# VectorE's order in the expert loop: the low part of half-chunk 10 placed behind the clip and SwiGLU of the second half

## The chip, the cores and the metric

The kernel runs on one core of a Trainium2 chip. The metric is the device time of one execution in microseconds, from its first to its last instruction with what lies around them. Times of a kernel are medians of several executions; the profile is one execution more.

## What is computed

One layer of a decoder, for 512 prompt tokens and 32 sample tokens (8 sequences of 4) that share the weights: windowed attention, a short convolution and memory attention side by side, then a mixture of experts with 32 experts, four of them for each token, then a last norm. The part around the change is the expert layer:

```python
def expert_block(args):
    xb, e = args
    h = xb @ w_gate_up[e] + b_gate_up[e]
    gate = jnp.minimum(h[:, 0::2], SWIGLU_LIMIT)
    up = jnp.clip(h[:, 1::2], -SWIGLU_LIMIT, SWIGLU_LIMIT)
    glu = gate * jax.nn.sigmoid(gate * SWIGLU_ALPHA)
    return ((up + 1.0) * glu) @ w_down[e] + b_down[e]
```

The model width and the width of the expert's hidden layer are both 1024. Weights are float32: 8 MB of gate and up and 4 MB of down for each expert.

## The kernel before, in words

**Stages.** After norms, projections, attention, output projection and router (up to about 345 us) the experts run one after another, 32 of them, each over at most 104 gathered rows (CAP). Further blocks for experts with more rows follow only where a flag asks for them; here they don't run. A last stage adds the norm and stores.

**Split products.** A float32 product is made from three products of rounded operands: each operand is split into a high part (a cast to fp32r, by ScalarE) and a low part (the float32 value less its high part, by VectorE), and TensorE adds high x high, low x high and high x low in PSUM (`products`, lines 1507 to 1509).

**Chunks.** An expert's 12 MB come as 6 chunks of 2 MB into the buffers `raw`, each two half-chunks, t = 0 to 11. Half-chunks 0 to 3 hold gate and up columns of the first half of the hidden layer, 4 to 7 those of the second half, 8 to 11 hold w_down. For every t ScalarE makes the high part (`high_part`, L689), VectorE the low part (`low_part`, L1137), and TensorE takes 12 matmuls for t below 8 and 12 for t from 8, then raises `w_used`. There are four `high` buffers, used in turn: the high part of t waits until TensorE has used t - 4. ScalarE works 3 half-chunks ahead.

**Between the two products.** When t = 3 (t = 7) is used, the first (second) half of the hidden layer stands in PSUM. ScalarE then runs `gate_sigmoid` (L702, L705), VectorE `clip_up` (L1143) and `swiglu` (L1150, which waits for the sigmoid, and L1153). TensorE transposes the result (`act_rows`, L1498; the first half inside the order after t = 5, the second inside t = 9), ScalarE makes its high part (`act_high`, L709), VectorE its low part (`act_low`, L1132). The products of w_down wait for `act_low` of the first half at t = 8 and of the second half at t = 10. At the end of t = 9 TensorE also transposes the next expert's rows (`x_rows`, L1489), which ScalarE and VectorE split (`x_high` L714, `x_low` L1127).

**VectorE's order** is written by hand. Each engine works through its own list of instructions, in which a wait stands ahead of what needs it. The function `expert` of VectorE steps through t; the table `AHEAD_T` says behind which step which low parts are made (numbers from 12 on belong to the next expert), apart from that of half-chunk 7, which stands inside step 4 and that of the next expert's half-chunk 0, which stands in step 10. Step 9 has no other work on VectorE. So its order from step 6 on is: act_low of half 1, low 9, low 10, clip and SwiGLU of half 2, low 11, act_low of half 2, low 0 of the next expert, x_low, low 1, low 2.

**The DMA queue** (SyncE) refills chunk q once both its half-chunks are used; ScalarE's high parts wait for the chunk's landing.

Of the kernel before, what the change touches and what calls it, by code (L numbers as in the profile page):

```python
# [111 lines left out]
def build(nc, x_prompt, x_sample, mem_prompt, cache_win_k, cache_win_v, win_kT, mem_kT, cache_mem_v,  # L112
# [4 lines left out]
    with ctx:  # L117
# [641 lines left out]
        def _(dv):  # L759
# [363 lines left out]
            def x_low(n):  # L1123
                for half in range(2):
                    hs = slice(half * 4, half * 4 + 4)
                    dv.wait_ge(sem("x_high"), n * 2 + (half + 1))
                    v.tensor_tensor(xL[:, hs, :], split(banks[half][:, 0:4 * CAP], 4), xH[:, hs, :], ALU.subtract).then_inc(sem("x_low"), 1)  # L1127
# [6 lines left out]
            def low_part(n, t):  # L1134

                dv.wait_ge(sem("w_high"), n * HALVES + (t + 1))
                v.tensor_tensor(low_w(t), raw_w(t), high_w(t), ALU.subtract).then_inc(sem("w_low"), 1)  # L1137
# [14 lines left out]
                dv.wait_ge(sem("up_ready"), m + 1)  # L1152
                v.scalar_tensor_tensor(out=u, in0=u, scalar=1.0, in1=g, op0=ALU.add, op1=ALU.mult).then_inc(sem("glu_ready"), 1)  # L1153

            AHEAD_T = {0: (3,), 1: (4,), 2: (5,), 3: (6,), 5: (8,), 6: (9,), 7: (10,), 8: (11,), 11: (13, 14)}

            def expert(n, k):
                for t in range(HALVES):
# [13 lines left out]
                    if t == 10:  # L1172
                        low_part(n + 1, 0)
                        x_low(n + 1)
                    for lead in AHEAD_T.get(t, ()):
                        low_part(n + lead // HALVES, lead % HALVES)
# [438 lines left out]
```

## Time and profile before

| what | value |
|---|---|
| median of 3 runs | 1611.83 us (1609.97 to 1612.02) |
| the profiled execution | 1607.12 us |
| its span, first to last instruction | 1605.3 us |
| mean granted TensorE clock | 0.965 |
| TensorE busy, share of the span | 92% |
| VectorE | 76% |
| ScalarE | 62% |

The span lies 1.8 us under the execution's own time, and that 4.7 us under the median of the runs. In a timeline the columns are start (us), duration (us), engine, line, operation, tile written <- tiles read, shapes, count, and in brackets the idle time of the engine just before and the instruction that ended it. Neighbours of one kind are merged into one row with their count and the time from the first start to the last end. PEld is the loading of weights into TensorE, which lies beside its matmuls.

### The profile page before, as it was taken

Reading aid. Unit: us, or ns where it says so; the run is one execution under the profiler, and the core shown is the slowest. Engines: PE = TensorE matmul, PEld = TensorE weight load, DVE = VectorE, ACT = ScalarE, POOL = GpSimd, SP = SyncE. Lnnn points to the kernel's source line nnn. Section 1 sums busy time; section 2 is a strip of 40 time slices with the busy share of each in tenths; the row PEclk is TensorE's granted clock in tenths of the full one; section 3 lists DMA queues with packets and bytes.
Section 4 is the critical chain, followed back from the end, with each engine's and each line's share of the span. In section 5 each row is a group of like instructions: output and inputs, shape, how many; then the busy total and the mean of one; then the engine's idle time right before and its main releaser. Section 6 shows DMA issues by size and latency. Waiting matters only on the chain.

```text
span 1605.3 us, 19091 instructions
## 1 busy us (share of the span) xinstructions
PE 1482.8 (92%) x6863; PEld 1080.0 (67%) x6863; DVE 1213.3 (76%) x1117; ACT 987.9 (62%) x927; POOL 257.8 (16%) x166
## 2 busy tenths in 40 slices
PE   6999799949999999999999999999999999999992
PEld 4877595436777777677777777777777777667772
DVE  3034305468888888888888888888888888888884
ACT  2023402127777777777777777777777777777774
POOL 2001300011112111111111211111111211111111
PEclk9999859969999999999999999999999999999996
DMA  9300307138999999999999999999999999999973
GB/s 348 152 5 0 132 0 305 78 120 296 355 339 346 348 345 338 348 335 360 355 344 346 349 342 337 346 345 339 349 343 342 346 349 340 345 343 350 348 290 134
DMA packets 52110, 462.90 MB, mean 288 GB/s; under 512 B 10498, under 2 KB 14548, under 8 KB 27028
## 3 DMA queue, kind: packets, MB, share of 16 engines
q1 hardware_dynamic: 40676, 441.39, 73.3%
q0 software_dynamic: 9360, 17.85, 5.1%
q10 hardware_dynamic: 2032, 3.12, 0.6%
q8 instruction: 24, 0.39, 0.1%
q14 instruction: 18, 0.15, 0.0%
HBM read 451.15 MB, written 22.04 MB: 295 GB/s over the span
## 4 chain that ended last, share of the span: by engine, by line
PE 67%; issue 6%; ACT 6%; DVE 4%; DMA 1%; POOL 0%; ACTq 0%; DVEq 0%; POOLq 0%
PE psum L1509 18%; PE psum L1507 18%; PE psum L1508 18%; PE psum L1455 4%; ACT high L689 4%; PE psum L1498 2%; PE psum L1522 2%; PE psum L1489 1%; DVE area L1153 1%; ACT area L702 1%; DVE area L1150 1%; PE psum L1535 1%; PE psum L1479 1%; PE psum L1438 1%; DVE low L1137 1%
## 5 line engine op out<-in xcount | busy, mean ns | idle before, releaser
L1137 DVE TENSOR_TENSOR low<-raw,high 128x2048 fp32r<-128x2048 f32 x387 | 883.4, 2290 | 146.2 <-ACT high L689 140.6
L689 ACT CAST high<-raw 128x2048 fp32r<-128x2048 f32 x387 | 731.1, 1909 | 129.2 <-PE psum L1509 116.8
L1507 PE MATMUL psum<-high,area_r 128*104 128x512 f32 x1536 | 608.4, 396 | 0.0
L1509 PE MATMUL psum<-low,area_r 128*104 128x512 f32 x1536 | 603.9, 393 | 0.0
L1508 PE MATMUL psum<-high,area_r 128*104 128x512 f32 x1536 | 603.6, 393 | 0.0
L1509 PEld LDWEIGHTS psum<-low,area_r 128*104 128x104 f32 x1536 | 257.9, 168 | 97.4
L1508 PEld LDWEIGHTS psum<-high,area_r 128*104 128x104 f32 x1536 | 258.4, 168 | 93.3
L1507 PEld LDWEIGHTS psum<-high,area_r 128*104 128x104 f32 x1536 | 258.4, 168 | 89.0
L490 POOL CAST pick_r<-area 64x104 fp32r (+1 forms) x33 | 74.6, 2262 | 545.8 <-PE psum L1509 545.7
L507 POOL DMA_INDIRECT area<-hn_tbl,idx_i x33 | 78.5, 2380 | 163.0 <-DVE idx_i L1120 157.4
L517 POOL DMA_INDIRECT y_tbl<-area,idx_i x32 | 52.0, 1624 | 317.2 <-ACT area L696 317.2
L1244 PE MATMUL psum<-ring 128*128 128x272 f32 x416 | 96.6, 393 | 0.0
L1244 PEld LDWEIGHTS psum<-ring 128*128 128x128 f32 x416 | 78.6, 190 | 18.5 <-issue 2.4
L709 ACT CAST area_r<-psum 128x416 fp32r<-128x416 f32 x64 | 32.2, 503 | 80.3 <-PE psum L1498 80.3
L702 ACT ACTIVATE area<-psum,cst 104x512 f32<-104x512 f32 x64 | 44.1, 689 | 53.5 <-PE psum L1509 53.5
L1498 PE MATMUL psum<-cst,area 104*128 104x104 f32 x256 | 35.1, 259 | 43.2 <-DVE area L1153 43.2
L1455 PE MATMUL psum<-area 128*128 128x512 f32 (+1 forms) x160 | 72.2, 606 | 2.0 <-DVE area L930 2.0
L1498 PEld LDWEIGHTS psum<-cst,area 104*128 104x128 f32 x256 | 26.8, 140 | 62.2 <-DVE area L1153 57.3
L696 ACT ACTIVATE area<-psum,area 104x512 f32<-104x512 f32 x64 | 40.5, 684 | 30.1 <-PE psum L1509 30.1
L1522 PE MATMUL psum<-bias_r,pick_r 128*104 128x512 f32 x128 | 54.9, 429 | 1.8 <-DVE area_r L1127 1.8
L816 DVE COPY area<-psum 128x272 f32<-128x272 f32 x13 | 5.7, 441 | 66.8 <-PE psum L1244 66.8
L714 ACT CAST area_r<-psum 128x416 fp32r<-128x416 f32 x66 | 30.3, 511 | 39.8 <-PE psum L1489 39.8
(196 smaller groups left out, 986.8 us busy)
## 6 DMA issues: line engine op xcount, KB each, us to landing
raw<-in_w_gate_up SPq DMA_DIRECT2D x130, 2048.0 KB, 10.5
raw<-in_w_down SPq DMA_DIRECT2D x64, 2048.0 KB, 7.9
ring<-in_w_in SPq DMA_DIRECT2D x1, 4096.0 KB, 37.5
area<-in_w_out SPq DMA_DIRECT2D x1, 4096.0 KB, 34.8
ring<-in_w_in SPq DMA_DIRECT2D x1, 3072.0 KB, 22.7
area<-in_x_prompt SPq DMA_DIRECT2D x4, 512.0 KB, 8.4
ring<-in_w_mem_kv SPq DMA_DIRECT2D x1, 2048.0 KB, 14.5
ring<-in_mem_kT SPq DMA_DIRECT2D x1, 2048.0 KB, 9.9
```

The lines of the kernel that those rows point to most:

```text
L490: nc.gpsimd.tensor_copy(pick_r[0:2 * NE, (k % 2) * CAP:(k % 2 + 1) * CAP], ptab[0:2 * NE, bass.ds(n, 1)].broadcast_to([2 * NE, CAP])).then ...
L507: nc.gpsimd.indirect_dma_start(xg[0:CAP, k % 2, :], None, hn_tbl[:, :], bass.IndirectOffsetOnAxis(ap=idx_i[0:CAP, k % UB:k % UB + 1].bitca ...
L689: nc.scalar.copy(high_w(t), raw_w(t)).then_inc(sem("w_high"), 1)
L702: nc.scalar.activation(gt[0:CAP, fh, :], banks[2 * fh][0:CAP, :], ACT.Relu, bias=limit[0:CAP], scale=-1.0).then_inc(sem("over_ready"), 1)
L1137: v.tensor_tensor(low_w(t), raw_w(t), high_w(t), ALU.subtract).then_inc(sem("w_low"), 1)
L1244: last = mm(banks[bank][:, 0:HALF], w_tile(Z_ORDER[i], k), xT0[:, k, half * HALF:(half + 1) * HALF], start=(k == 0), stop=(k == KD - 1))
L1455: last = mm(banks[half * 3 + part][0:n, :], zT[:, t, j * P:j * P + n], wo[:, t, half * 512:(half + 1) * 512], start=(t == tiles[0]), stop= ...
L1498: last = tr(banks[6 + fh][:, q * CAP:(q + 1) * CAP], up[0:CAP, fh, q * P:(q + 1) * P], ident[0:CAP, 0:CAP])
L1507: mm(bank, high, wh, start=False, stop=False)
L1508: mm(bank, low, wh, start=False, stop=False)
L1509: return mm(bank, high, wl, start=False, stop=stop)
L1522: mm(bank, pick, bias_r[:, q * 512:(q + 1) * 512], start=True, stop=False)
```

## The change

In `AHEAD_T` the entry 7: (10,) becomes 8: (10,), and 8: (11,) becomes 9: (11,). The entry of a step is worked off at that step's end. So the low part of half-chunk 10 is made at the end of step 8, behind `clip_up(n, 1)` and `swiglu(n, 1)`; that of half-chunk 11 stands behind them as before, now with low 10 ahead of it. No instruction is added or removed, and the orders of the other engines are untouched.

```diff
-            AHEAD_T = {0: (3,), 1: (4,), 2: (5,), 3: (6,), 5: (8,), 6: (9,), 7: (10,), 8: (11,), 11: (13, 14)}
+            AHEAD_T = {0: (3,), 1: (4,), 2: (5,), 3: (6,), 5: (8,), 6: (9,), 8: (10,), 9: (11,), 11: (13, 14)}
```

## Rows read from the trace of the kernel before

**Rows 1.** The page: busy time of each engine, and TensorE's granted clock in 40 slices.
```profile
PE 1482.8 (92%) x6863; PEld 1080.0 (67%) x6863; DVE 1213.3 (76%) x1117; ACT 987.9 (62%) x927; POOL 257.8 (16%) x166
...
PEclk9999859969999999999999999999999999999996
```

**Rows 2.** Busy time by windows, one expert; last columns granted clock, DMA share, GB/s.
```profile
903.99:942.03 38.04, 36.74 (x172) 26.90 (x171) 33.65 (x26) 28.03 (x22) 6.63 (x4) 1.00 0.94 346
```

**Rows 3.** TensorE's waits, whole span: us in total, times, longest.
```profile
PE psum L1498 <- DVE area L1153: 43.2, 32, 2.5
```

**Rows 4.** Timeline of VectorE, one expert, 910 to 938 us.
```profile
910.25 0.69 DVE L1153 SCALAR_TENSOR_TENSOR area<-area 104x512 f32<-104x512 f32 x1
...
913.95 2.29 DVE L1137 TENSOR_TENSOR low<-raw,high 128x2048 fp32r<-128x2048 f32 x1 [0.31 <-ACT high L689]
916.57 2.29 DVE L1137 TENSOR_TENSOR low<-raw,high 128x2048 fp32r<-128x2048 f32 x1 [0.33 <-ACT high L689]
918.78 0.68 DVE L1143 TENSOR_SCALAR area<-psum 104x512 f32<-104x512 f32 x1
919.38 0.68 DVE L1150 SCALAR_TENSOR_TENSOR area<-psum,area 104x512 f32<-104x512 f32 x1
920.10 0.69 DVE L1153 SCALAR_TENSOR_TENSOR area<-area 104x512 f32<-104x512 f32 x1
920.72 2.29 DVE L1137 TENSOR_TENSOR low<-raw,high 128x2048 fp32r<-128x2048 f32 x1
922.96 0.59 DVE L1132 TENSOR_TENSOR area_r<-psum,area_r 128x416 fp32r<-128x416 f32 x1
...
925.66 1.08 DVE L1127 TENSOR_TENSOR area_r<-psum,area_r 128x416 fp32r<-128x416 f32 x2
926.86 4.64 DVE L1137 TENSOR_TENSOR low<-raw,high 128x2048 fp32r<-128x2048 f32 x2
...
933.21 4.49 DVE L1137 TENSOR_TENSOR low<-raw,high 128x2048 fp32r<-128x2048 f32 x2 [1.10 <-ACT high L689]
```

**Rows 5.** Timeline of ScalarE, the same expert, 914 to 930 us.
```profile
914.63 1.91 ACT L689 CAST high<-raw 128x2048 fp32r<-128x2048 f32 x1 [0.70 <-PE psum L1509]
917.38 0.69 ACT L702 ACTIVATE area<-psum,cst 104x512 f32<-104x512 f32 x1 [0.84 <-PE psum L1509]
918.16 0.72 ACT L705 ACTIVATE area<-area,cst 104x512 f32<-104x512 f32 x1
918.79 3.73 ACT L689 CAST high<-raw 128x2048 fp32r<-128x2048 f32 x2
922.42 0.50 ACT L709 CAST area_r<-psum 128x416 fp32r<-128x416 f32 x1
...
927.26 1.92 ACT L689 CAST high<-raw 128x2048 fp32r<-128x2048 f32 x1 [0.43 <-PE psum L1509]
```

**Rows 6.** Timeline of TensorE, the same expert, 911 to 930 us.
```profile
911.00 0.58 PE L1498 MATMUL psum<-cst,area 104*128 104x104 f32 x4 [1.30 <-DVE area L1153]
...
921.79 0.52 PE L1498 MATMUL psum<-cst,area 104*128 104x104 f32 x4
...
923.55 0.88 PE L1489 MATMUL psum<-cst,area 104*128 104x104 f32 x8
924.20 0.46 PE L1507 MATMUL psum<-high,area_r 128*104 128x512 f32 x1
...
929.84 0.39 PE L1522 MATMUL psum<-bias_r,pick_r 128*104 128x512 f32 x1
```

**Rows 7.** The instructions of line 1132: durations in ns, minimum, median, maximum.
```profile
L1132 DVE TENSOR_TENSOR area_r<-psum,area_r x64: 578/584/594, 380.0 to 1570.0; 128x416 fp32r<-128x416 f32 x64
```

**Rows 8.** Timeline of ScalarE, the last expert.
```profile
1565.14 0.72 ACT L705 ACTIVATE area<-area,cst 104x512 f32<-104x512 f32 x1
```

**Rows 9.** Timeline of TensorE, the last expert.
```profile
1571.21 0.46 PE L1507 MATMUL psum<-high,area_r 128*104 128x512 f32 x1
```

**Rows 10.** Busy time by windows, columns as in rows 2, an earlier stage.
```profile
243.00:247.00 4.00, 3.89 (x6) 1.71 (x7) 3.74 (x8) 3.18 (x6) 0.00 (x0) 0.57 0.97 334
```

## The prediction

> **What bounds the kernel now.** I read the page first: TensorE is busy for 92% of the span, and its clock is at the upper level in nearly every slice [rows 1]. The windows of one expert then give the period of the loop: 38.04 us, of which TensorE is busy for 36.74 at a granted clock of 1.00, so 1.30 us are idle [rows 2]. 32 such periods are about 1217 us, three quarters of the kernel. TensorE's waits say where these 1.30 us lie: one wait per expert, 32 in all and 43.2 us together, at the transposes of the first half (L1498), for the SwiGLU of that half [rows 3]. There is no wait at the second half's transposes, and none at half-chunk 10. In the loop any new wait of TensorE is therefore paid in full, unless it shortens this one; and any wait of another engine is free until it reaches TensorE. So the question is only when TensorE's two inputs from VectorE in this stretch come: the SwiGLU of the second half (for the transposes at 921.79) and act_low of the second half (for half-chunk 10 at 924.20) [rows 6].
>
> **The order before, with its slacks.** VectorE makes low 9 (913.95 to 916.24), low 10 (916.57, released by its high part, to 918.86), clip (918.78), the two steps of SwiGLU (919.38, 920.10 to 920.79), low 11 (920.72), act_low (922.96 to 923.55) [rows 4]. Half-chunk 7 is used at about 917.35: ScalarE's first step of the gate, which waits for the same count as the clip, starts at 917.38 [rows 5]. So low 10 does two things. It fills VectorE's time while TensorE finishes half-chunk 7 and ScalarE makes the sigmoid (which ends at 918.16 + 0.72 = 918.88 [rows 5]), and it leaves only low 11 between SwiGLU and act_low. The slacks: SwiGLU is ready at 920.79, 1.00 us ahead of the transposes; act_low is ready at 923.55, 0.65 us ahead of half-chunk 10's first matmul [rows 4, 6].
>
> **What the change removes.** Clip and SwiGLU no longer stand behind low 10. That brings SwiGLU's end from 920.79 to about 920.3 (below). I cost this at nothing: TensorE comes to these transposes in its own order at 921.79 and didn't wait there. What follows them, ScalarE's high part of the same data at 922.42, starts as soon as ScalarE's two high parts are through (918.79 + 3.73 = 922.52, neighbours overlapping by a tenth) and not earlier [rows 5]. Nobody else reads the SwiGLU. Low 10 itself comes later, but TensorE wants it only at 924.20, and low 11 another 12 matmuls (2.8 us) later.
>
> **What it adds: one low part, and the idle time that it filled, between the sigmoid and act_low.** The new order, step by step, with the spacings of starts of rows 4:
> - low 9 ends at 916.24. VectorE idles until the clip's wait ends. The trace has no clip that was released by TensorE; the nearest row is ScalarE's gate step on the same count, 917.38. The value matters little: SwiGLU's first step waits for the sigmoid until 918.88, and a clip that started as late as 918.3 would still be out of its way (clip to SwiGLU is 0.60).
> - SwiGLU's first step starts 0.03 us behind the sigmoid's end (as low 10 does behind its high part: 914.63 + 1.91 = 916.54, and 916.57 [rows 4, 5]): 918.91.
> - Its second step 0.72 later (919.38 to 920.10): 919.63. Low 10 then 0.62 later (920.10 to 920.72): 920.25.
> - Low 11 2.20 later (two low parts back to back take 4.49, of which 2.29 are the second [rows 4]): 922.45. Its high part, the first of the pair that starts at 918.79, is long there.
> - act_low again 2.20 later: 924.65. Its high part is there (922.42 + 0.50 [rows 5]). It takes 0.59, with 578 to 594 ns over all 64 [rows 7]: ready at 925.24.
> - TensorE starts 0.06 behind VectorE's end (910.25 + 0.69 = 910.94, and 911.00 [rows 4, 6]): 925.30.
>
> From the sigmoid's end that is a chain of 0.03 + 0.72 + 0.62 + 2.20 + 2.20 + 0.59 + 0.06 = 6.42 us. Before, half-chunk 10 began at 924.20; its delay is 1.10 us. A restart after a wait costs a little more: the four transposes behind the existing wait take 0.58, those without a wait 0.52 [rows 6]. I add 0.06, which makes 1.16 us for each expert. In the last expert the sigmoid ends at 1565.86, the chain at 1572.28, and half-chunk 10 began at 1571.21: 1.07 in place of 1.10 [rows 8, 9]. So the experts are alike from end to end.
>
> **What is late next, and whether the delay is given back.** VectorE is 1.69 us later at act_low (924.65 against 922.96), TensorE 1.16. x_low ends at 926.74 + 1.69 = 928.43, and TensorE wants it with the next expert's first half-chunk, from 929.84 + 1.16 on. Low 1 of the next expert ends at about 926.86 + 2.29 + 1.69 = 930.84, and its half-chunk begins 12 matmuls behind that. Low 2 waits for its high part in the order before, which waits for half-chunk 10 (ScalarE, 927.26 [rows 5]) and moves with TensorE. By the next low 3, before which VectorE idled for 1.10 us [rows 4], the 0.53 us by which VectorE is further behind than TensorE are made up. So the delay is neither passed on twice nor given back. The wait that exists, at the first half's transposes, hangs on a chain that starts when TensorE has used half-chunk 3: it moves with TensorE and keeps its length. ScalarE and GpSimd have the same orders; SyncE's refills, one after each pair of half-chunks, come later with TensorE, and no high part waited for a transfer in these rows. Over a longer period the same 12 MB ask for less than the 346 GB/s of now [rows 2]. No DMA is issued by what is moved.
>
> **The sum.** 32 x 1.16 = 37.1 us. On the profiled execution, 1607.12 + 37.1 = 1644.2 us; on the median of the runs, 1611.83 + 37.1 = 1648.9 us.
>
> **Bounds.** The unknown costs are the release of SwiGLU and the restart of TensorE. At the low end nothing is added at the restart and the chain is the last expert's: 1.07, or 0.95 if the wakes of rows 4 and 6 overlap what I counted. At the high end the first matmuls of half-chunk 10 pay the transposes' exposure and one matmul's spacing more (0.06 + 0.23), and 0.1 at the sigmoid: 1.10 + 0.39 = 1.49. Times 32 that is 30 to 48 us, or 1642 to 1660. I take 1.16, near the low end, because the existing wait [rows 6] is the same kind of restart.
>
> **Rivals.**
> - *Not slower: act_low isn't late.* The mechanism is the gain that the order could bring: if TensorE at 921.79 was held by SwiGLU after all, its coming 0.5 us earlier is worth up to 0.47 x 32 = 15 us, 1597 us; if it wasn't held, nothing, 1611.8. Either needs act_low ready by 924.14, that is a chain 1.1 us shorter than mine, half a low part. Against it stand the 64 waits that there would be where rows 3 show 32, and the fixed durations of rows 4 and 7. 5% (2 faster, 3 same).
> - *The delay is taken whole.* If the 1.69 us of VectorE's delay reach TensorE in place of 1.16 (because a later input has less slack than I read), the price is 1.69 x 32 = 54 us, 1666 us. It decides if x_low or a low part of the next expert has under 0.5 us of slack; I found 2 us and more. 4%.
> - *The clock falls.* With a second idle gap of about 1.1 us in each period the granted clock could fall to its lower level (1.2 GHz) after half-chunk 10. Where the earlier stage restarts from the lower level, a stretch of 4 us shows 0.57 [rows 10], so most of 4 us at half rate, about 1.7 us of lost matmul time. With 32 of them, 37 + 55 = 92 us, 1704 us. Against it: the existing gap of 1.30 us leaves 1.00 in the same window [rows 2], and the two gaps lie 13 us apart with solid matmuls between. 3%. The Trainium skill (TensorE: Matmul & The Clock Gate, Part 1) has the rule behind this rival: an array that has idled is put back to half rate, and sustained work releases it. By that rule a change that adds idle gaps can cost more than the gaps; in the trace of before the gap that is there already does not bring it about.
> - *The change doesn't do what it says.* Low 11 stood behind SwiGLU before as well, so only low 10 moves. If the entry of step 8 were worked off ahead of the SwiGLU, nothing would change: 1611.8. The code has it behind. 1%.
>
> **How the numbers follow.** The forecast has 87%: 1648.9 us. The range runs over its bounds with a little to spare below for a median that comes out nearer to the profiled execution's level, 1640 to 1660; it leaves out the rivals' 13% and a few per cent of the forecast. Slower by over 0.2%, about what a measurement of this kernel can tell from no change: 87 + 4 + 3 = 94%. Within 0.2%: 3 + 1 = 4%. Faster: 2%.
>
> **What the profile after would show.** TensorE's waits get a second line: 32 waits at line 1507 of half-chunk 10 for L1132, of 1.1 to 1.3 us each beyond the spacing, some 35 us in total (less as the profile counts idle time from the modelled end of the matmul before, which lies up to 0.2 us late). The line of 43.2 us stays. VectorE idles for about 1.1 us before the clip (released by TensorE) and 0.3 to 0.9 us before SwiGLU (released by L705). The expert's period becomes 39.2 us in place of 38.04, with the clock at 1.00. The prediction is wrong if act_low lies behind 924.2 in the same frame without TensorE waiting for it, if the wait at L1498 becomes shorter, or if the period grows by another amount than that wait.

## The result and the profile after

The changed kernel takes 1645.0 us (median of 4 runs, 1644.2 to 1646.0) against 1611.4 us for the kernel before in the same comparison (1610.0 to 1612.0): a ratio of 1.0214 with a 95% interval of 1.0202 to 1.0226, so it is 33 to 36 us slower. Forecast were 1648.9 us and a range of 1640 to 1660.

Of the page of after, the line of busy times and TensorE's granted clock (compare rows 1). TensorE has the same 6863 instructions at the same clock, on a span longer by 39 us. Its busy time is 9.1 us longer all the same; most of that, 0.19 us for each expert, is the modelled end of the row transposes, which lay under the next matmul before and now lies ahead of a gap (in the windows of one expert 36.93 in place of 36.74):

```profile
span 1644.0 us, 19091 instructions
...
PE 1491.9 (91%) x6863; PEld 1081.7 (66%) x6863; DVE 1208.3 (73%) x1117; ACT 989.7 (60%) x927; POOL 313.4 (19%) x166
...
PEclk9999759969999999999999999999999999999996
```

One expert of after by windows, columns as in rows 2 (here from clip to clip, in rows 2 from gate step to gate step). The period has grown from 38.04 to 39.19 us, the clock is 1.00, the transfers run at 335 in place of 346 GB/s:

```profile
924.00:963.19 39.19, 36.93 (x172) 26.94 (x171) 33.49 (x26) 28.05 (x23) 8.37 (x4) 1.00 0.91 335
```

TensorE's waits in after (total us, times, longest), the answer to rows 3: the old wait is there unchanged, and a new one stands beside it.

```profile
PE psum L1498 <- DVE area L1153: 43.5, 32, 2.5
PE psum L1507 <- DVE area_r L1132: 29.1, 32, 0.9
```

VectorE's waits in after. The second and third line are new, and they are the time that low 10 used to fill. The first was 140.6 us in before; it is shorter mainly because low 10 no longer waits 0.33 us in each expert for its high part:

```profile
DVE low L1137 <- ACT high L689: 124.3, 130, 3.8
...
DVE area L1143 <- PE psum L1509: 35.9, 32, 1.1
...
DVE area L1150 <- ACT area L705: 26.7, 32, 0.9
```

The timelines of one expert of after, VectorE first, then ScalarE's sigmoid, then TensorE (compare rows 4, 5 and 6):

```profile
932.58 2.29 DVE L1137 TENSOR_TENSOR low<-raw,high 128x2048 fp32r<-128x2048 f32 x1 [0.31 <-ACT high L689]
936.00 0.69 DVE L1143 TENSOR_SCALAR area<-psum 104x512 f32<-104x512 f32 x1 [1.13 <-PE psum L1509]
937.54 0.69 DVE L1150 SCALAR_TENSOR_TENSOR area<-psum,area 104x512 f32<-104x512 f32 x1 [0.85 <-ACT area L705]
938.27 0.69 DVE L1153 SCALAR_TENSOR_TENSOR area<-area 104x512 f32<-104x512 f32 x1
938.88 4.49 DVE L1137 TENSOR_TENSOR low<-raw,high 128x2048 fp32r<-128x2048 f32 x2
943.28 0.58 DVE L1132 TENSOR_TENSOR area_r<-psum,area_r 128x416 fp32r<-128x416 f32 x1
```

```profile
936.79 0.72 ACT L705 ACTIVATE area<-area,cst 104x512 f32<-104x512 f32 x1
```

```profile
940.41 0.52 PE L1498 MATMUL psum<-cst,area 104*128 104x104 f32 x4
...
942.17 0.88 PE L1489 MATMUL psum<-cst,area 104*128 104x104 f32 x8
944.00 0.47 PE L1507 MATMUL psum<-high,area_r 128*104 128x512 f32 x1 [0.95 <-DVE area_r L1132]
```

Read them from the sigmoid on. It ends at 936.79 + 0.72 = 937.51. SwiGLU starts 0.03 later, low 10 and low 11 follow back to back, act_low is ready at 943.28 + 0.58 = 943.86, and TensorE starts half-chunk 10 at 944.00. It would have started at 942.82, 0.65 us behind the start of the row transposes, as at 923.55 and 924.20 in rows 6. So this expert loses 1.18 us there. It is one of those that lose most: over all experts half-chunk 10 starts 1.69 to 1.83 us behind the start of the row transposes, 1.79 on average, where before has 0.65 or 0.66 throughout. The average loss is 1.13 us.

**A sharper measure than the median.** The stages ahead of the loop vary by some microseconds from one execution to the next (here the loop of after starts 3.2 us later than that of before). Below, the *loop time* is the time from the first to the last start of the 1536 matmuls of high x high, which the row of that line gives. For before and for after:

```profile
L1507 PE MATMUL psum<-high,area_r x1536: 388/393/632, 356.6 to 1576.1; 128*104 128x512 f32 x192
```

```profile
L1507 PE MATMUL psum<-high,area_r x1536: 388/392/628, 359.8 to 1615.1; 128*104 128x512 f32 x192
```

1219.5 us became 1255.3 us: 35.8 us, or 1.12 us for each of 32 experts.

### The profile page after: what moved, and what is told of

Read it like the earlier page. It is cut to its first block, busy times and chain, and to the rows that moved or that the text cites. A ratio compares the mean times of both kernels' runs of the same rounds, so it can differ in the third digit from the quotient of the medians.

```text
span 1644.0 us, 19091 instructions
## 1 busy us (share of the span) xinstructions
PE 1491.9 (91%) x6863; PEld 1081.7 (66%) x6863; DVE 1208.3 (73%) x1117; ACT 989.7 (60%) x927; POOL 313.4 (19%) x166
## 4 chain that ended last, share of the span: by engine, by line
PE 52%; DVE 13%; issue 10%; ACT 8%; DMA 1%; DVEq 0%; POOL 0%; ACTq 0%; POOLq 0%
PE psum L1507 15%; PE psum L1509 14%; PE psum L1508 14%; DVE low L1137 6%; PE psum L1455 4%; ACT high L689 4%; DVE area L1150 3%; ACT area L702 3%; DVE area L1153 2%; PE psum L1522 2%; ACT area L705 2%; DVE area_r L1132 1%; PE psum L1498 1%; PE psum L1479 1%; PE psum L1438 0%
## 5 line engine op out<-in xcount | busy, mean ns | idle before, releaser
L1507 PE MATMUL psum<-high,area_r 128*104 128x512 f32 x1536 | 608.1, 396 | 29.1 <-DVE area_r L1132 29.1
L490 POOL CAST pick_r<-area 64x104 fp32r (+1 forms) x33 | 130.0, 3939 | 545.8 <-PE psum L1509 545.7
L709 ACT CAST area_r<-psum 128x416 fp32r<-128x416 f32 x64 | 32.4, 506 | 80.3 <-PE psum L1498 80.3
L1498 PE MATMUL psum<-cst,area 104*128 104x104 f32 x256 | 35.1, 259 | 43.5 <-DVE area L1153 43.5
L1143 DVE TENSOR_SCALAR area<-psum 104x512 f32<-104x512 f32 x64 | 44.0, 688 | 35.9 <-PE psum L1509 35.9
L1498 PEld LDWEIGHTS psum<-cst,area 104*128 104x128 f32 x256 | 26.8, 140 | 62.5 <-DVE area L1153 57.6
L1150 DVE SCALAR_TENSOR_TENSOR area<-psum,area 104x512 f32<-104x512 f32 x64 | 44.0, 688 | 26.7 <-ACT area L705 26.7
L471 POOL TENSOR_TENSOR ring<-ring,small 128x1024 f32<-128x1024 f32 (+3 forms) x10 | 24.8, 2481 | 174.6 <-DVE small L856 174.6
```

What stands on the lines that cost most here:

```text
L490: nc.gpsimd.tensor_copy(pick_r[0:2 * NE, (k % 2) * CAP:(k % 2 + 1) * CAP], ptab[0:2 * NE, bass.ds(n, 1)].broadcast_to([2 * NE, CAP])).then ...
L1150: v.scalar_tensor_tensor(out=g, in0=banks[2 * fh][0:CAP, :], scalar=LIMIT, in1=g, op0=ALU.min, op1=ALU.mult).then_inc(sem("glu_made"), 1)
L1498: last = tr(banks[6 + fh][:, q * CAP:(q + 1) * CAP], up[0:CAP, fh, q * P:(q + 1) * P], ident[0:CAP, 0:CAP])
L1507: mm(bank, high, wh, start=False, stop=False)
```

## The experiments

The theory: what counts is when act_low of the second half is ready, and that is a chain from the sigmoid on, with a slack of about half a microsecond in the kernel before. The rivals: that the move of clip and SwiGLU, or idle time of VectorE as such, costs; that all work of VectorE in the loop counts; that a later input of TensorE pays.

| kernel | median, us | ratio to before (95%) | loop time, us | new wait at half-chunk 10, us |
|---|---|---|---|---|
| before | 1611.4 | 1 | 1219.5 | none |
| after | 1645.0 | 1.0202 to 1.0226 | 1255.3 | 29.1 |
| act_low ahead of low 11 | 1611.7 | 1.0000 to 1.0024 | 1219.6 | none |
| low 10 split | 1610.7 | 0.9997 to 1.0023 | 1220.3 | none |
| low 10 between clip and SwiGLU | 1615.1 | 1.0023 to 1.0048 | 1225.0 | none listed |
| before, one instruction more | 1610.5 | 0.9989 to 1.0017 | 1219.5 | none |
| before, two more | 1629.2 | 1.0096 to 1.0140 | 1238.5 | 12.6 |
| after, one more | 1664.8 | 1.0326 to 1.0367 | 1273.7 | 48.1 |
| low 7 behind SwiGLU | 1561.0 | 0.9673 to 0.9705 | 1169.6 | none |
| the same, in after | 1593.6 | 0.9873 to 0.9906 | 1204.4 | 29.0 |
| the same, act_low ahead of low 11 | 1560.9 | 0.9670 to 0.9703 | 1169.3 | none |

The kernel before had medians of 1609.7 to 1611.4 us in the four comparisons; each ratio is to its own.

Experiments 1 to 3 are built on the changed kernel, 4 and 5 on the kernel before.

**1. act_low ahead of low 11, on top of the change.**

```diff
-            AHEAD_T = {0: (3,), 1: (4,), 2: (5,), 3: (6,), 5: (8,), 6: (9,), 8: (10,), 9: (11,), 11: (13, 14)}
+            AHEAD_T = {0: (3,), 1: (4,), 2: (5,), 3: (6,), 5: (8,), 6: (9,), 8: (10,), 11: (13, 14)}
...
                     if t in (6, 10):
                         act_low(n, (t - 6) // 4)
                     if t == 10:
+                        low_part(n, 11)
                         low_part(n + 1, 0)
                         x_low(n + 1)
```

> The changed kernel with one more move: act_low of the second half ahead of low 11 (clip, SwiGLU, low 10, act_low, low 11). Theory (two low parts between SwiGLU and act_low make TensorE wait at half-chunk 10): one low part is left, VectorE is ready at 922.5 in the frame of before and act_low starts when its high part is there (922.96, as before), so no wait at half-chunk 10; low 11 is ready at about 925.8, 1.2 us ahead of its matmuls. 1611 us, period 38.05. Rival (the clip and SwiGLU in their new place, or VectorE's new idle time, cost by themselves): stays near 1645. Rival (a later input pays: x_low or a low part of the next expert now comes 2.2 us later than before): a new wait at the next expert's first half-chunks, between 1611 and 1645.

The cost is gone: a loop time of 1219.6 us. Clip and SwiGLU are in their new place, and VectorE has the same idle time ahead of them as in after. Its timeline shows why that no longer matters: act_low now waits for its own high part again.

```profile
921.32 0.69 DVE L1143 TENSOR_SCALAR area<-psum 104x512 f32<-104x512 f32 x1 [1.13 <-PE psum L1510]
922.86 0.69 DVE L1150 SCALAR_TENSOR_TENSOR area<-psum,area 104x512 f32<-104x512 f32 x1 [0.85 <-ACT area L705]
923.59 0.69 DVE L1153 SCALAR_TENSOR_TENSOR area<-area 104x512 f32<-104x512 f32 x1
924.20 2.28 DVE L1137 TENSOR_TENSOR low<-raw,high 128x2048 fp32r<-128x2048 f32 x1
926.89 0.59 DVE L1132 TENSOR_TENSOR area_r<-psum,area_r 128x416 fp32r<-128x416 f32 x1 [0.41 <-ACT area_r L709]
927.40 4.48 DVE L1137 TENSOR_TENSOR low<-raw,high 128x2048 fp32r<-128x2048 f32 x2
```

The first rival falls with it: neither the place of clip and SwiGLU nor VectorE's idle time costs anything. So does the rival of a later input: low 11, low 0 and x_low come later than in before, and no wait appears. And so does a rival that wasn't named ahead, the longer time of GpSimd (its busy time grows by 55.6 us in after, see the last section): in this kernel it is longer still, 322.9 us against 313.4 (other instructions of GpSimd take longer there, the cast of the last section less), and the time is that of before.

**2. Half the dose: low 10 split in two.**

```diff
-            AHEAD_T = {0: (3,), 1: (4,), 2: (5,), 3: (6,), 5: (8,), 6: (9,), 8: (10,), 9: (11,), 11: (13, 14)}
+            AHEAD_T = {0: (3,), 1: (4,), 2: (5,), 3: (6,), 5: (8,), 6: (9,), 9: (11,), 11: (13, 14)}
...
                     if t == 8:
+                        low_half(n, 10, 0)
                         clip_up(n, 1)
                         swiglu(n, 1)
+                        low_half(n, 10, 1)
```

`low_half` is `low_part` on 1024 of the 2048 columns; only the second half reports low 10 as made.

> Half a dose: low 10 made in two instructions of 1024 columns, the first ahead of the clip, the second behind SwiGLU; low 11 as in both kernels. Theory: the first half fills VectorE's wait, the chain behind the sigmoid is 1.07 us shorter than in the changed kernel, so act_low is ready at about 924.2 in the frame of before, with half-chunk 10 at 924.20: a wait of 0.1 us, 1611 + 3 = 1614 us (1611 to 1619). If the cost were proportional to the work moved, without a slack: about 1628. If it hung on the clip's and SwiGLU's place: 1645.

Loop time 1220.3 us, 0.8 over before where 3 were expected: nearly nothing for half of the move. The slack takes that half; a cost in proportion (1237 us) is excluded.

**3. Low 10 between clip and SwiGLU.**

```diff
-            AHEAD_T = {0: (3,), 1: (4,), 2: (5,), 3: (6,), 5: (8,), 6: (9,), 8: (10,), 9: (11,), 11: (13, 14)}
+            AHEAD_T = {0: (3,), 1: (4,), 2: (5,), 3: (6,), 5: (8,), 6: (9,), 9: (11,), 11: (13, 14)}
...
                     if t == 8:
                         clip_up(n, 1)
+                        low_part(n, 10)
                         swiglu(n, 1)
```

> The changed kernel with low 10 between clip and SwiGLU of the second half, so behind the wait for half-chunk 7 and in the place of the wait for the sigmoid. Theory (the cost is the idle time of VectorE that low 10 no longer fills, 1.13 us ahead of the clip and 0.85 ahead of SwiGLU, less the slack): the second of the two is filled again. From the clip's release at 917.38: low 10 at 917.98, SwiGLU at 920.19 and 920.91, low 11 at 921.52, act_low at 923.72, ready at 924.31, TensorE at 924.45 against 924.20: 0.25 us for each expert, 1610 + 8 = 1618 us. SwiGLU is ready at 921.60, 0.2 us ahead of the transposes. If what counts is only that low 10 stands behind the clip: 1645.

Low 10 still stands behind the wait for half-chunk 7, but fills the wait for the sigmoid:

```profile
922.74 0.69 DVE L1143 TENSOR_SCALAR area<-psum 104x512 f32<-104x512 f32 x1 [1.12 <-PE psum L1510]
923.35 2.28 DVE L1137 TENSOR_TENSOR low<-raw,high 128x2048 fp32r<-128x2048 f32 x1
925.55 0.68 DVE L1150 SCALAR_TENSOR_TENSOR area<-psum,area 104x512 f32<-104x512 f32 x1
926.27 0.69 DVE L1153 SCALAR_TENSOR_TENSOR area<-area 104x512 f32<-104x512 f32 x1
926.88 2.28 DVE L1137 TENSOR_TENSOR low<-raw,high 128x2048 fp32r<-128x2048 f32 x1
929.08 0.58 DVE L1132 TENSOR_TENSOR area_r<-psum,area_r 128x416 fp32r<-128x416 f32 x1
```

Loop time +5.5 us, 0.17 for each expert where 0.25 was expected. In this expert half-chunk 10 starts 0.88 us behind the start of the row transposes in place of 0.65, and the transposes are listed with 0.88 us. A delay that short lies within the modelled end of the instruction before it, so the list of waits doesn't show it; only the loop time does.

**4. One instruction more in the kernel before.**

```diff
+                    if t == 10:
+                        v.tensor_scalar(spare[0:CAP, :], banks[3][0:CAP, :], LIMIT, -LIMIT, ALU.min, ALU.max)
                     if t in (6, 10):
                         act_low(n, (t - 6) // 4)
```

`spare` is a tile that nobody reads.

> The kernel before with one more VectorE instruction (a clip of 104x512 from PSUM into a spare tile, spacing 0.60 us) directly ahead of act_low of the second half. Nothing else changes. Theory: VectorE is free at 922.92 there, act_low then starts at 923.52 in place of 922.96 and is ready at 924.11, TensorE at 924.25 against 924.20: the slack takes nearly all of it. +0 to +4 us, 1611 to 1615. If every VectorE instruction in the loop counts (VectorE bound): +19 us, 1630.

Nothing: 1219.5 us. The instruction is there (VectorE, line 1172) and puts act_low off by 0.57 us (2.81 behind low 11's start, 2.24 in rows 4). That just about uses up the slack: half-chunk 10 starts 0.67 us behind the row transposes on average over the experts, where 0.65 is the undisturbed distance.

```profile
924.70 2.29 DVE L1138 TENSOR_TENSOR low<-raw,high 128x2048 fp32r<-128x2048 f32 x1
926.91 0.68 DVE L1172 TENSOR_SCALAR area<-psum 104x512 f32<-104x512 f32 x1
927.51 0.58 DVE L1133 TENSOR_TENSOR area_r<-psum,area_r 128x416 fp32r<-128x416 f32 x1
```

**5. Two more in the kernel before.** The same edit with a second spare tile.

> The kernel before with two more VectorE instructions (spacing 0.60 us each) directly ahead of act_low of the second half, where one cost nothing. Theory: the slack there is 0.65 us less the 0.14 us that TensorE needs to start again; act_low starts at 924.12 in place of 922.96 and is ready at 924.71, TensorE starts at 924.85 against 924.20: 0.65 us for each expert, +20 us, 1631 us, with 32 new waits at half-chunk 10. If VectorE's work there is free altogether: no change.

Loop time +19.0 us, 0.59 for each expert. TensorE's waits and its timeline at half-chunk 10:

```profile
PE psum L1512 <- DVE area_r L1134: 12.6, 32, 0.4
```

```profile
934.16 0.88 PE L1494 MATMUL psum<-cst,area 104*128 104x104 f32 x8
935.45 0.47 PE L1512 MATMUL psum<-high,area_r 128*104 128x512 f32 x1 [0.41 <-DVE area_r L1134]
```

It starts 1.29 us behind the row transposes' start where 0.65 is the undisturbed distance: 0.64 late, of which 0.41 is listed as idle. That is also why the total of 29.1 us in after is less than its 35.8 us.

**6. One instruction more in the changed kernel.** The edit of experiment 4.

> The changed kernel with the same additional instruction in the same place. Theory: the slack is used up, so all of its 0.60 us reach TensorE in each of 32 experts: +19 us on the changed kernel, 1664 us, and the waits at half-chunk 10 grow from 29 to 48 us. Rival (the clock falls when the gap becomes longer, 1.6 us in place of 0.9): granted clock below 1.00 in the windows behind the gap, and well over 1664.

Loop time +18.4 us over after, 0.58 of the instruction's 0.60 us, and the wait grows from 29.1 to 48.1 us:

```profile
PE psum L1510 <- DVE area_r L1133: 48.1, 32, 1.5
```

With 4 and 5 this is the whole curve: the same 0.6 us are free in the kernel before, cost 19.0 us as a second one there, and 18.4 us in the changed kernel. The gap in TensorE's work is now 1.5 us, and the clock is still 1.00 in the window from 400 to 1540 us, so the rival of a falling clock doesn't appear here either.

**7. The other half of the expert: low 7 behind SwiGLU.** This is the same kind of move on the kernel before, at the wait that bounds it.

```diff
                     if t == 4:
                         clip_up(n, 0)
-                        low_part(n, 7)
                         swiglu(n, 0)
+                        low_part(n, 7)
```

> The kernel before with the mirrored move in the first half: low 7 placed behind clip and SwiGLU of the first half, where it stood between clip and SwiGLU. Here the low part is not between SwiGLU and something late: its high part is made behind the sigmoid, so low 7 can't start before 907.3 in any order, while SwiGLU could run from 905.5. Theory: SwiGLU is ready at 906.9 in place of 910.94, TensorE's wait at the transposes (L1498, 43 us in all) goes, its restart with it: 911.00 becomes 909.54, 1.46 us for each expert, 1611 - 47 = 1565 us, period 36.6. Low 7 keeps its time and has 3 us of slack. Rival (the same rule as in the change, a low part behind SwiGLU costs): slower than 1611. Rival (transfers bind, their share is 0.94 now and would be 0.98): ScalarE's high parts wait for DMA, 1575 to 1600.

1561.0 us against 1610.7, 3.1% faster (2.95 to 3.27); loop time -49.9 us, 1.56 for each expert where 1.46 was expected. Half of the 0.10 more is TensorE's restart: what follows the transposes starts 0.35 us behind them after the wait (911.00 and 911.35 in before) and 0.30 without it (927.61 and 927.91 here). The other half wasn't traced. The wait of 43.2 us is gone from TensorE's list. VectorE, and TensorE's transposes of the first half, which have no idle time ahead of them any more:

```profile
923.44 0.68 DVE L1143 TENSOR_SCALAR area<-psum 104x512 f32<-104x512 f32 x1
924.04 0.68 DVE L1150 SCALAR_TENSOR_TENSOR area<-psum,area 104x512 f32<-104x512 f32 x1
924.75 0.69 DVE L1153 SCALAR_TENSOR_TENSOR area<-area 104x512 f32<-104x512 f32 x1
925.40 4.49 DVE L1137 TENSOR_TENSOR low<-raw,high 128x2048 fp32r<-128x2048 f32 x2
929.81 0.58 DVE L1132 TENSOR_TENSOR area_r<-psum,area_r 128x416 fp32r<-128x416 f32 x1
```

```profile
927.61 0.52 PE L1498 MATMUL psum<-cst,area 104*128 104x104 f32 x4
```

Low 7 starts at 925.40, 1.96 us behind the clip's start, and in before 1.93 behind it (907.32 and 905.39 in the same view): it loses nothing, because its high part isn't there sooner. SwiGLU no longer stands behind that wait. The transfers go along, at 352 GB/s from 400 to 1540 us where before had 346; the rival that they bind (1575 to 1600 us) is out.

**8 and 9. The same in the changed kernel, and with act_low ahead of low 11.**

> The same move of low 7 in the changed kernel. Theory: the two waits of TensorE are independent, each hangs on a chain that starts with TensorE's own half-chunk (3 and 7), so the gain is the same, 1645 - 47 = 1598 us, and the wait at half-chunk 10 stays at 29 us. Rival (the waits cover each other, VectorE being behind by the same amount in both): a difference to the run without the change well off 34 us.

> Low 7 behind SwiGLU of the first half, low 10 behind SwiGLU of the second, and act_low of the second half ahead of low 11. Theory: no wait of TensorE is left in the loop, as with low 7 alone: 1565 us; VectorE's low 11 and x_low are later but in time. If low 11 or x_low now comes too late in the shorter period: a few us over low 7 alone.

Measured: 1593.6 and 1560.9 us, each 4 us under what was expected, as in experiment 7. The two waits are independent to within 1 us: low 7's move gains 50.9 us in the changed kernel (1255.3 to 1204.4) and 49.9 in the kernel before; the change costs 34.8 us with low 7 moved and 35.8 without. With act_low ahead of low 11 as well, the loop takes 1169.3 us, as with low 7 alone: with low 7 alone TensorE is busy for 1131 of the 1140 us from 400 to 1540, so hardly anything is left to win in the loop by VectorE's order.

## Why the prediction was right, point by point

- **The bound.** TensorE, with one wait per expert and a slack of 0.65 us at half-chunk 10 [rows 2, 3, 6]: right. Experiments 4 and 5 measure the slack: 0.6 us more are free, 1.2 us cost 0.59. The 0.65 us run up to the end of act_low; TensorE's start behind that end, 0.14 us, comes off, which leaves 0.51 to use in the expert shown.
- **What it removes is worth nothing.** Right: ScalarE's high part (L709) starts 3.5 us behind the sigmoid's end in after (941.04 and 937.51) as in before (922.42 and 918.88 [rows 5]), although SwiGLU is ready sooner.
- **The chain from the sigmoid on, 6.42 us.** Measured 6.49 (937.51 to 944.00). The spacings on VectorE are exact: 5.77 us to act_low's start, predicted and measured. The start of TensorE behind act_low takes 0.14 us where the row of L1498 had shown 0.06.
- **The restart, 0.06 us.** It costs 0.01: the first matmul lasts 0.47 and not 0.46. The bound from the transposes [rows 6] was the wrong neighbour; these are another kind of matmul. The two errors, +0.08 and -0.05, nearly cancel, and that is luck.
- **Nothing is passed on or given back.** Right. From half-chunk 10's start to the next row transposes an expert takes 37.42 us in before and 37.40 in after, on average. Behind half-chunk 10 the order is back in step: VectorE's idle time before low 3 is 0.91 us where it was 1.10 [rows 4]. Experiments 6 and 8 show that the delay neither grows nor hides behind the other wait.
- **The sum.** 32 x 1.16 = 37.1 us; the loop time grew by 35.8. For each expert 1.16 us were forecast and 1.12 measured. The forecast was worked out on one expert, and the same expert of after loses 1.18 us at half-chunk 10, the average one 1.13. The medians differ by 33.6 us, within 33 to 36; the 2 us between the two measures lie inside the variation of single runs and weren't traced further.
- **The rivals.** Not slower: excluded. The delay taken whole (54 us): excluded. The clock: a second gap of 0.95 us, and of 1.5 us in experiment 6, beside the old one of 1.30 left it at 1.00. The Trainium skill's rule (TensorE: Matmul & The Clock Gate, Part 1) that an idle array is put back to half rate did not come into play with gaps of this size in any run here.
- **Total of the new wait.** Forecast were some 35 us, less the modelled ends: 29.1. For each expert that is 0.9 us of listed idle time; the loss beyond the usual spacing, for which I named 1.1 to 1.3, is 1.13 on average. I had also called the prediction wrong if the period grew by another amount than the wait. It grew by 1.15 us, which fits the loss, but not the listed 0.9 us; that sign should have named the loss.

## What to carry to other kernels

When independent work stands on an engine ahead of instructions that wait, ask two things of it: could it start only later anyway, and does something late stand behind the pair? Low 10 was ready to run while clip and sigmoid weren't, so ahead of them it was free, and behind them it pushed act_low past its slack of half a microsecond: 36 us over 32 experts. Low 7 was the reverse case, an instruction that had to wait for its own input and held a SwiGLU that was ready; the same kind of move there gained 50 us.

## What the runs showed of the hardware that wasn't expected

GpSimd's busy time grew from 258 to 313 us with no instruction added. It is one cast of 64x104 elements (`pick_r`, L490) that starts when TensorE has used half-chunk 8. Durations in ns, minimum, median and maximum, in before, after, the split of experiment 2, act_low ahead of low 11, and low 10 between clip and SwiGLU:

```profile
L490 POOL CAST pick_r<-area x33: 267/2387/2475, 341.8 to 1529.7; 64x104 fp32r x28, 64x104 fp32r<-64x104 f32 x5
```

```profile
L490 POOL CAST pick_r<-area x33: 268/4112/4174, 345.0 to 1566.4; 64x104 fp32r x28, 64x104 fp32r<-64x104 f32 x5
```

```profile
L490 POOL CAST pick_r<-area x33: 267/3038/3101, 342.0 to 1530.5; 64x104 fp32r x28, 64x104 fp32r<-64x104 f32 x5
```

```profile
L490 POOL CAST pick_r<-area x33: 267/1902/2214, 345.7 to 1533.6; 64x104 fp32r x28, 64x104 fp32r<-64x104 f32 x5
```

```profile
L490 POOL CAST pick_r<-area x33: 266/267/2216, 344.9 to 1537.9; 64x104 fp32r x28, 64x104 fp32r<-64x104 f32 x5
```

The cast alone takes 0.27 us. In the last kernel it starts at 926.10, beside SwiGLU's first step (L1150, which has one input in PSUM), and takes that. In after it starts at 939.36, beside low 10 and low 11, and ends at 943.50:

```profile
939.36 4.14 POOL L490 CAST pick_r<-area 64x104 fp32r x1 [17.55 <-PE psum L1509]
```

That is 0.13 us behind the end of low 11 (938.88 + 4.49 = 943.37). Low 10 alone lets it go earlier, as experiment 1 shows, where a gap follows it: there the cast ended at 926.61, 0.13 us behind the end of low 10 (924.20 + 2.28 = 926.48).

```profile
924.68 1.93 POOL L490 CAST pick_r<-area 64x104 fp32r x1 [15.21 <-PE psum L1510]
```

So two low parts back to back held it to the end of both. The Trainium skill (SBUF — State Buffer, Who interferes with whom) has GpSimd and VectorE share a port pair of which the one in possession keeps the other out, among others for a VectorE instruction with two SBUF inputs beside a GpSimd instruction that reads SBUF. The low part and the cast are such a pair, and the trace agrees: 2.39 us beside one low part, 4.11 beside two, 0.27 beside an instruction with a PSUM input. It costs nothing in this kernel, as nobody wants the cast before the next expert. By an estimate from these rows (4.11 less 0.27) a GpSimd instruction on a critical path would pay some 3.8 us there, for a change that only moves VectorE's work.
